# Spreading the convolution's taps over the attention cycles, a later GpSimd convolution, own tiles for the sample and an earlier first down-projection load, in a hybrid decoder step

## The reference, cut to what matters

```python
def stick_breaking(q, k, v, q_pos, k_pos, bias):
    z = einsum('bqhd,bkhd->bhqk', q, k) * HEAD_DIM ** -0.5 + bias
    mask = k_pos[None, :] < q_pos[:, None]
    log_keep = where(mask, log_sigmoid(-z), 0.0)
    log_between = cumsum(log_keep, axis=3, reverse=True) - log_keep
    a = where(mask, exp(log_sigmoid(z) + log_between), 0.0)
    return einsum('bhqk,bkhd->bqhd', a, v)
def conv_module(glu_ext, w, b, ln_g, ln_b):      # causal depthwise conv of width 31 over 512 channels
    y = depthwise_conv(glu_ext, w) + b
    return silu(layernorm(y, ln_g, ln_b))
for x in (prompt, sample):                        # they share all weights
    h = modulate(rmsnorm(x, norm_mix), shift1, scale1)
    q, k, v, glu = split(h @ w_in)                # q and k RMS-normed per head, glu = ca * sigmoid(cg)
    att = stick_breaking(q, past and own k, past and own v)    # 8 heads of 64
    x = x + gate1 * concat(att, conv_module(glu)) @ w_out
    h = modulate(rmsnorm(x, norm_ffn), shift2, scale2)
    x = x + gate2 * moe(h)                        # 16 experts, 2 of one group for each token
```

## Time and profile before

| what | us |
|---|---|
| median of 3 runs | 1249.69 |
| lowest to highest run | 1249.06 to 1250.74 |
| the profiled execution, its own time | 1246.21 |
| span of the profiled execution, first to last instruction | 1244.5 |
| PE matmul busy | 1150.9 (92%) |
| DVE busy | 602.6 (48%) |
| ACT busy | 337.2 (27%) |
| GpSimd busy | 252.1 (20%) |

### The profile page before, as it was taken

The page is one execution under the profiler, slowest core; times in us unless marked ns, Lnnn a source line. Parts: engine busy times, 40 slices in busy tenths (PEclk is TensorE's granted clock), DMA queues, the critical chain, the costliest instruction groups (busy, mean ns, idle before and its releaser), DMA issues.

```text
span 1244.5 us, 19620 instructions
## 1 busy us (share of the span) xinstructions
PE 1150.9 (92%) x6769; PEld 539.9 (43%) x6769; DVE 602.6 (48%) x1161; ACT 337.2 (27%) x713; POOL 252.1 (20%) x312
## 2 busy tenths in 40 slices
PE   6999999999978798998999974899999999999996
PEld 3444444444435566665544443233333333333332
DVE  0010867787689988887965357021221221221212
ACT  2132222122037788887312221000000000000000
POOL 2011101111059500000010001123223233232322
PEclk8999999999988999999999995899999999999999
DMA  9933333322246475654843245997688876977653
GB/s 358 335 134 102 103 102 106 105 81 84 87 150 214 135 225 162 219 159 152 318 144 118 85 150 185 356 398 280 229 283 335 300 286 241 360 252 251 218 215 128
DMA packets 115859, 253.37 MB, mean 204 GB/s; under 512 B 15054, under 2 KB 29518, under 8 KB 114760
## 3 DMA queue, kind: packets, MB, share of 16 engines
q1 hardware_dynamic: 94241, 208.42, 48.1%
q0 software_dynamic: 17568, 39.35, 9.1%
q10 hardware_dynamic: 3984, 4.72, 1.1%
HBM read 399.77 MB, written 39.22 MB: 353 GB/s over the span
## 4 chain that ended last, share of the span: by engine, by line
PE 79%; DVE 6%; DMA 6%; issue 4%; ACT 3%; SPq 0%; POOL 0%; ACTq 0%; DVEq 0%; POOLq 0%
PE bank L1780 20%; PE bank L1457 20%; PE bank L1794 10%; PE bank L1648 8%; PE bank L1437 3%; DMA big<-in_w_gate_dram 2%; PE bank L1491 2%; PE bank L1531 2%; PE bank L1770 1%; PE bank L1313 1%; PE bank L1541 1%; PE bank L1519 1%; DMA big<-in_w_down_dram 1%; DVE big L2060 1%; DMA mid<-in_w_ada_dram 1%
## 5 line engine op out<-in xcount | busy, mean ns | idle before, releaser
L1780 PE MATMUL bank<-big,mid 128*64 128x512 f32 x1232 | 282.2, 598 | 2.0 <-DMA big<-in_w_gate_dram 1.9
L1457 PE MATMUL bank<-big 128*128 128x512 f32 x560 | 249.2, 598 | 0.1
L1457 PEld LDWEIGHTS bank<-big 128*128 128x128 f32 x560 | 103.6, 190 | 131.3 <-issue 131.3
L1953 DVE SCALAR_TENSOR_TENSOR cvT<-low,cw,cvT 128x256 f32<-128x256 f32 x360 | 158.3, 516 | 0.1
L1780 PEld LDWEIGHTS bank<-big,mid 128*64 128x64 f32 x1232 | 87.9, 137 | 159.7 <-issue 158.6
L1794 PE MATMUL bank<-big,mid 128*64 128x512 f32 x608 | 133.7, 592 | 1.1 <-DMA big<-in_w_down_dram 1.1
L2060 DVE TENSOR_TENSOR_SCAN big<-big 128x513 f32<-128x513 f32 (+4 forms) x96 | 91.3, 991 | 15.8 <-ACT big L1086 15.6
L2480 DVE TENSOR_TENSOR xt<-xt,bank 128x512 f32<-128x512 f32 x20 | 13.8, 688 | 152.3 <-ACT xt L1255 152.3
L1794 PEld LDWEIGHTS bank<-big,mid 128*64 128x64 f32 x608 | 44.0, 137 | 87.7 <-issue 87.7
L2499 DVE TENSOR_TENSOR mid<-bank,low 128x512 f32<-128x512 f32 x38 | 24.5, 686 | 115.2 <-PE bank L1794 85.6
L795 POOL TENSOR_TENSOR st<-st,mhalf 128x16 f32<-128x16 f32 (+1 forms) x9 | 25.2, 2801 | 252.6 <-DVE st L1984 243.8
(11 more groups left out here) (341 smaller groups left out, 1344.2 us busy)
## 6 DMA issues: line engine op xcount, KB each, us to landing
big<-in_w_gate_dram SPq DMA_DIRECT2D x42, 2048.0 KB
big<-in_w_up_dram SPq DMA_DIRECT2D x41, 2048.0 KB
big<-in_w_down_dram SPq DMA_DIRECT2D x41, 2048.0 KB
low<-in_w_ada_dram SPq DMA_DIRECT2D x32, 512.0 KB, 4.2
low<-in_cache_v_dram SPq DMA_DIRECT2D x64, 256.0 KB
big<-in_w_in_dram SPq DMA_DIRECT2D x8, 1280.0 KB, 17.2
xt<-in_x_prompt_dram SPq DMA_DIRECT2D x16, 512.0 KB, 4.8
mid<-in_w_ada_dram SPq DMA_DIRECT2D x8, 1024.0 KB, 13.9
```

Of the source, the lines that this page charges most:

```text
L1457: mm = pe.matmul(bank[:, 4 if cc == 2 else cc, :], hT[:, s, k, :], w_in_sb[:, k, cc * 512:(cc + 1) * 512], start=(k == 0), stop=(k == KD - 1))
L1780: mm = pe.matmul(bank[half, 2 * s + w, :], xgT[:, s, k, half], moving, start=(k == 0), stop=(k == KD - 1))
L1953: c.put(V.scalar_tensor_tensor(out, src, cw[:, ch, tap:tap + 1], out, ALU.mult, ALU.add))
```

## The change

Five edits. (1) The sample's q and k, v and gated rows get tiles of their own in `mid` (columns 7168 to 7679, which neither `kT` nor the second half of the key pages covers). The waits of ACT and DVE for stores of those tiles go, and `evac_page(0)`, which overwrites the prompt's tiles, waits for the prompt's stores alone and no more for those of the sample; SP waits for the sample's before it loads w_out over them. (2) The ten instructions of `conv_part(NTP - 1, 3)` ahead of cycle 0 go, and come back two a cycle at the end of the cycles 0 to 4. (3) `TAPS_BY` changes. In taps a cycle, cycles 0 to 15, it was 2 2 2 2 2 1 2 1 2 1 2 1 2 1 2 1 and is 1 1 1 1 2 2 2 2 2 2 2 2 2 2 1 1. (4) GpSimd begins the sample's convolution once `pv_mm` is at 8, so when eight units have been multiplied by their values. (5) At the start of the experts SP issues the first pass's down load as soon as the up weights have landed, ahead of the next pass's gate load, and GpSimd issues the second gather of rows only when the first has landed.

```diff
--- before.py
+++ after.py
@@ tiles of the projection @@
         kT_t = mid[:, 6656:7168]
+        smp_qk = mid[:, 7168:7168 + 2 * P]
+        smp_v = mid[:, 7168 + 2 * P:7168 + 3 * P]
+        smp_glu = mid[:, 7168 + 3 * P:7168 + 4 * P]
@@ sync: store_kv @@
-                    sp.dma_start(new_conv_prompt[0, 0], glu_t[P - TAIL:P, s, :]).then_inc(S["conv_st"], 16)
+                    sp.dma_start(new_conv_prompt[0, 0], glu_t[P - TAIL:P, s, :]).then_inc(kv_st[s], 16)
@@ sync: store_sample @@
-                sp.dma_start(ks_out.rearrange("b (j n) -> j b n", j=4), qk_t[:, s, P:2 * P]).then_inc(kv_st[s], 16)
+                sp.dma_start(ks_out.rearrange("b (j n) -> j b n", j=4), smp_qk[:, P:2 * P]).then_inc(kv_st[s], 16)
...
@@ sync: before the loads of w_out @@
             sp.wait_ge(S["qkT_st"], 32 * NTP)
+            sp.wait_ge(S["conv_st"], 16 * 5)
             sp.wait_ge(S["s_mm"], DB)
@@ sync: first loads of the experts @@
                          cond=e1[0] != 1).then_inc(S["spare_in"], 16)
+            sp.wait_ge(wu_in[1], 16)
+            load_w(wd_sb, w_down, wd_in, e0, (0, None))
             sp.wait_ge(S["g_mm"], 1)
             settle(sp)
             sp.sem_inc(wg_in[0], 16)
             sp.dma_start(wg_sb[:, 1, :, :], w_gate[0, bass.ds(e1[1], 1), :, :].rearrange("a (k p) n -> p (a k) n", p=P),
                          cond=e1[1] != e0[1]).then_inc(wg_in[1], 16)
-            load_w(wd_sb, w_down, wd_in, e0, (0, None))
@@ gpsimd @@
             pool.wait_ge(S["glu_sb"], NT)
             pool.wait_ge(S["mm_chunk"], MM_ALL)
+            pool.wait_ge(S["pv_mm"], NTP)
...
             fetch_x(0)
+            pool.wait_ge(xg_in[0], 16)
             fetch_x(1)
@@ scalar @@
-            act.wait_ge(kv_st[s], 32 * (NTP // 2))
-            nc.scalar.activation(v_t[:, s, 0:P], bank[:, 0, 2 * P:3 * P], ACT.Copy).then_inc(S["v_done"], 1)
+            nc.scalar.activation(smp_v, bank[:, 0, 2 * P:3 * P], ACT.Copy).then_inc(S["v_done"], 1)
...
                 if n == 0:
-                    act.wait_ge(kv_st[0], 32 * 5)
-                    act.wait_ge(kv_st[1], 32 * 4)
-                    act.wait_ge(S["conv_st"], 16 * 6)
+                    act.wait_ge(kv_st[0], 32 * (NTP // 2))
+                    act.wait_ge(kv_st[1], 32 * (NTP // 2) + 16)
@@ vector @@
-            dve.wait_ge(kv_st[s], 32 * (NTP // 2))
-            V.tensor_tensor(qk_t[:, s, 0:2 * P].rearrange("p (h d) -> p h d", d=HD),
+            V.tensor_tensor(smp_qk.rearrange("p (h d) -> p h d", d=HD),
...
             dve.sem_inc(S["qbd_done"], 1)
-            conv_part(NTP - 1, 3)
             c.reset()
...
-            TAPS_BY = [2 * cy - max(0, (cy - 4) // 2) for cy in range(CYCLES + 1)]
+            TAPS_BY = [max(cy, min(2 * cy - 4, CYCLES + cy - 6)) for cy in range(CYCLES + 1)]
...
                 if cy == CYCLES - 1:
                     ln_sum2(0)
+                if cy < CW - LATE_TAP:
+                    conv_taps(NTP // 2 - 2, (2, 3), LATE_TAP + cy, LATE_TAP + cy + 1)
                 for tap in range(TAPS_BY[cy], TAPS_BY[cy + 1]):
                     conv_tap(tap)
```

More of the change, by code:

```diff
@@ L557, in store_sample @@
                                          [[TAIL * CC, DB], [CC, DS], [1, P]]),
-                                 glu_t[NS * j:NS * (j + 1), s, 0:P]).then_inc(S["conv_st"], 16)
+                                 smp_glu[NS * j:NS * (j + 1), :]).then_inc(S["conv_st"], 16)
             def store_mods(w):
@@ L801, in _ @@
                     pool.wait_ge(S["const_in"], 16 * N_CONST)
-                normed = qk_t[:, t % 2, 0:2 * heads * HD].rearrange("p (w h d) -> p w h d", w=2, d=HD)
+                normed = (qk_t[:, t % 2, :] if t < NTP else smp_qk).rearrange("p (w h d) -> p w h d", w=2, d=HD)
                 pool.tensor_tensor(normed, normed, qkw[:, :, :].unsqueeze(2).broadcast_to([P, 2, heads, HD]), ALU.mult)\
@@ L1156, in _ @@
                         act.wait_ge(S["qkT_st"], 32 * NTP)
-                        act.wait_ge(kv_st[1], 32 * (NTP // 2))
+                        act.wait_ge(kv_st[1], 32 * (NTP // 2) + 16)
                     else:
@@ L1363, in turn_post @@
                 for ch in range(NCH if t < NTP else 1):
-                    mm = pe.transpose(bank[:, 7, ch * P:(ch + 1) * P], glu_t[:, s, ch * P:(ch + 1) * P], identf[:, :])
+                    gated = glu_t[:, s, ch * P:(ch + 1) * P] if t < NTP else smp_glu
+                    mm = pe.transpose(bank[:, 7, ch * P:(ch + 1) * P], gated, identf[:, :])
                 mm.then_inc(S["post_ps"], 1)
@@ L1381, in turn_sample_qk @@
                 for j in range(2):
-                    pe.transpose(bank[:, 5 + j, 0:P], qk_t[:, NTP % 2, j * P:(j + 1) * P], identf[:, :])\
+                    pe.transpose(bank[:, 5 + j, 0:P], smp_qk[:, j * P:(j + 1) * P], identf[:, :])\
                         .then_inc(S["post_ps"], 1)
@@ L2009, in _ @@
             dve.wait_ge(S["post_ps"], 3 * (NTP - 2) + 1)
-            V.tensor_tensor(glu_t[:, s, 0:P], bank[:, 3, 0:P], sg_t[:, s, 0:P], ALU.mult)\
+            V.tensor_tensor(smp_glu, bank[:, 3, 0:P], sg_t[:, s, 0:P], ALU.mult)\
                 .then_inc(S["glu_done"], 1)
```

2 lines of the change are left out of this document (1 added, 1 removed).

## The result

The changed kernel takes 1259.07 us (median of 4 runs, 1257.11 to 1260.9) against 1249.38 for the kernel before in the same comparison: ratio 1.0085, 95% interval 1.0063 to 1.0107. It is slower by about 9.7 us, and the time lies outside the predicted range.

The account below looks back on a forecast made before the run. The prediction took PE, 79% of the chain that ended last, as the bound. Its terms 0 - 3.3 + 4.5 - 1.6 = -0.4 us took the median 1249.69 to 1249.3 us, range 1243.0 to 1253.7.

Parts of the forecast that it names:

- The start of attention: Edits 1 and 2: PE turns 7.3 us earlier, then waits for sequence 1's first page at half speed; net 0.
- The pause at 422.46: PE's wait for the sample's stick-breaking on DVE goes, with GpSimd silent and fewer taps: 3.3 us gained.
- The same work in the cycles 4 to 8: GpSimd's convolution, moved there, slows DVE and makes new PE pauses in cycles 7 and 9: 4.5 us lost (0 to 7.8).
- The experts: Edit 5: down load uses a free gap, gate lands about as before, down wait at 826.32 goes: 1.6 us gained.
- DVE becomes the bound from cycle 5 on: Rival: extra taps, late taps and GpSimd meet on DVE in the cycles from 5 on; 1253.6 us, chance 0.24.
- The key pages don't hold PE: Rival: at 386 PE finds sequence 1's pages ready, so the start's 7.3 us stay; 1242.0 us, chance 0.10.
- GpSimd is hidden: Rival: GpSimd's work in cycles 4 to 8 costs nothing, so the 4.5 us become 0; 1244.8 us, chance 0.24.

Follow-up runs that it names:

- stage_later: The changed kernel with ACT issuing head pair 1's staging (1.5 MB) in cycle 2 instead of cycle 1: 1253.6 us, ratio 1.0048.
- u_pool: The changed kernel without GpSimd's wait, so the sample's convolution starts right at the end of the projection as before: 1250.8 us, ratio 1.0014.
- u_taps: The changed kernel with the taps as before (ten late taps ahead of attention, old table), GpSimd still waiting: 1252.9 us, ratio 1.0030.
- no_smp2: The changed kernel with 30 of the 31 taps of the sample's convolution left out on GpSimd: 1252.4 us, ratio 1.0030.
- before_down: The kernel before with only the first down load moved, issued behind up instead of behind the gate load: 1252.2 us, ratio 1.0015.
- own_tiles: The kernel before with edit 1 alone, the sample's own tiles: 1248.8 us, ratio 1.0006.
- the four combinations: Changed kernel, key pages ahead of values, GpSimd not waiting, experts' start as before; variously with old taps, two pages, later staging: 1245.9, 1250.2, 1244.0, 1241.1 us.

## Why the prediction was wrong, step by step

**The start of attention, taken as 0 (range -4.1 to +0.9): +2.0.** The mechanism was right: turn at 369.27, SP's issue at 386.99 unmoved, PE standing still for it. Two things were off. The landing was taken from the median of the rows of before, 5.8 us; it took 6.9, since ACT's staging had moved ahead too. The prediction had this in a sentence beside the sum, at 0.5 us later than before, a figure without a working; the sum left it out. PE came to the page 0.3 us later than before (393.92, 393.58), and stage_later puts the price of the staging at 2.7 us. And the half-speed stretch behind the wait was 10.2 us (389.9 to 400.1), not the 6.7 of the earlier trace rows. It is moved as much as it is new: in 360 to 380 the granted clock was 0.66 in before and 0.83 now, in 380 to 400 it was 0.92 and is 0.75; but before, PE stood still in much of it, and now it works (6.09 us busy in those 10.2).

**The pause at 422.46, -3.3: -1.7.** The pause went whole, as predicted, and would have given 3.3: the same two cycles take 28.1 us in six of the experiments. In the profiled execution a half-speed stretch at 427.4 took 1.5 back.

**The same work in the cycles 4 to 8, +4.5 (0 to 7.8): +7.3.** The mechanism was right; the credit and the clock were mis-sized. The interference as a whole came out well, by luck: I took 3.9 cycles of 2.9 us, 11.3; up to the pause it was 10.7, in fewer and dearer cycles. GpSimd's 62 instructions took 43 us (440.51 to 483.4), 3.1 cycles, and a cycle beside them cost 4.1. Both misreadings come in good part from one instruction in the window of the earlier trace rows. GpSimd, then DVE, in before:

```profile
396.05 8.57 POOL L818 TENSOR_TENSOR cvT<-cvT,big 128x128 f32<-128x128 f32 x1
```

```profile
402.40 1.25 DVE L2060 TENSOR_TENSOR_SCAN big<-big 128x256 f32<-128x256 f32 x2
403.58 0.72 DVE L2070 TENSOR_TENSOR big<-big 128x256 f32<-128x256 f32 x2
```

While that one is recorded, the DVE instructions are as fast as alone; in the changed kernel, beside GpSimd's usual pace, the same two groups took 1.71 (457.57) and 1.16 us (459.20). So the 17 instructions in 14.5 us were too few for GpSimd's pace, and the 2.9 us, with these two groups slowed like the others, would have been 3.8. The credit was too large: of the 6.6 us free and 3.1 of lead that I set against it over four cycles, 3.2 and 2.1 could be used ahead of the one instruction that PE waits for, while the interference lies there nearly whole. That makes PE's turn 5.8 us late. The 2.1 us for `ln_sum` were right in size (two scans of 128x513 took 4.45 us at 485.10, 2.34 without GpSimd) and fell behind the pause. The other 1.5 of the 7.3 is the clock: I counted idle time only, but the pause came with 6.8 us at half speed (482.0 to 488.8), and from PE's turn to its next L1560 it took 22.6 us instead of 21.1 in u_pool. I had allowed such a loss for the wait for the page and for no other. u_pool, u_taps and no_smp2 say that it is the sum of GpSimd and taps. I placed the new pauses in the cycles 7 and 9 with 1 to 3 us each; it was cycle 7 alone. Of the Trainium skill's page "SBUF — State Buffer" (who interferes with whom) the traces show the direction and not the harshest reading: eight tap instructions grow from 3.25 to 4.68 us beside GpSimd, by 1.4 us, while GpSimd was busy 3.97 us of that stretch (475.63 to 480.23).

**The experts, -1.6 (-2.5 to -0.3): +3.4.** The wrong sign, and the step that failed is the overlap: the first down load was to vanish in the free time ahead of the gate load. First the gap: 3.2 us were to be free ahead of gate, 2.0 were, since the second gather made up land later; "it can't cost" was looked at where its rows are used and not at what it runs beside. Then the overlap: I let the 1.9 us by which the down load exceeds the gap vanish into "where it did, give or take 1", but they add to gate, and more than in full: 2.3 us in before, 3.4 to 4.2 in the changed kernel, where PE's pause grew from 5.8 to 9.3 us. Last, the 1.06 us at 826.32 was put down to the first down load by the tensor's name; it belongs to the second.

**No term: +1.5 and about +1.4.** The half-speed stretches at 546.9 and in the tail of the program (L1856's 48 matmuls at 1233.34 take 6.87 us; L1850's in before 5.40) come without a longer pause ahead of them than in before. before_down, which is before in every instruction of attention, had the same 1.5 us in cycle 8 to the end, so the change isn't needed for it. But one profile of each kernel can't say how often it comes: 105.3 us stand in the changed kernel and seven of its eight variants that aren't combinations, 103.8 in before, own_tiles, no_smp2 and the four combinations. I read these stretches as belonging to the execution, with the profiled one of before, 3.2 us under its median, as one with few of them; that would be most of the difference between the 13.6 us of the traces and the 9.7 of the medians. It is argued and not shown.

Of the rivals, "DVE becomes the bound from cycle 5 on" is what happened. Its place was right and its price, 1253.6, was 5.5 us low, for the clock and for the experts. "The key pages don't hold PE" and "GpSimd is hidden" are refuted by 8.49 us at 393.92 and 5.35 at 483.76.

What stays open: what makes the clock fall at 427.4 or 546.9, where PE had the same work and the same small pauses as in before; and why the down load costs gate more than its own size less the gap. No run here varied that.

## What to carry to other kernels

Freeing an engine is worth what is ready behind the wait: here 7 us of earlier start turned into a longer wait for a page whose issue nobody had moved, and only moving that issue and the competing staging made it 7 us of gain. A load put ahead of another in the same queue delayed it here by at least its own size less the gap that was really free (2.3 to 4.2 us measured, 1.6 to 3.1 by that sum), and that gap has to be taken from when its predecessor lands in the new order. Free time on an engine counts only where it lies ahead of the instruction that someone waits for, and a longer pause on TensorE should be charged with its half-speed stretch too: 5.35 us of standing still cost 7.0 here, while the 3.18 us in before cost 3.3. A window that gives the price of interference has to be looked through instruction by instruction, since one odd record in it spoiled both pace and price.

## What the runs showed of the hardware

Staging of 1.5 MB on ACT's queue delayed a page on SP's queue by 2.7 us (6.93 against 4.23 us from its issue to PE's first use). Beside GpSimd's 128x128 instructions the same 50 DVE instructions of two attention cycles were busy 33.08 us instead of 24.81. A part of what a pause costs is the clock: 5.35 us of idle time cost 7.0 between the marks on both sides of it. With the same attention instructions, the time from cycle 8 to its end was 103.8 us in some executions and 105.3 in others, the difference being one stretch of 3.4 us at a granted clock of 0.50.
